# VectorE's share of a delta rule step, dealt out over the slots

## The chip, the cores and the metric

One core of a Trainium2 chip runs the whole program in one launch. The metric is the device time of one execution in microseconds (us); the number of record is the median of three executions. Beside them stands one profiled execution, whose span is the stretch that the trace covers.

## What is computed

Three blocks run one after the other on 1024 tokens of width 1024. The change touches one stage of the first block only: a bidirectional gated delta rule with 4 heads of width 128, computed in chunks. This is its core, cut short:

```python
def gated_delta_chunked(q, k, v, g, beta):
    gc = jnp.cumsum(g, axis=-1)
    gamma = jnp.exp(jnp.where(lower, gc[..., :, None] - gc[..., None, :], -jnp.inf))
    kb = k * beta[..., None]
    a_mat = jnp.where(strict, jnp.einsum('bhncd,bhnsd->bhncs', kb, k) * gamma, 0.0)
    t_mat = a_mat + jnp.eye(C)
    u = triangular_solve(t_mat, v * beta[..., None])
    w = triangular_solve(t_mat, kb * jnp.exp(gc)[..., None])
    qk = jnp.einsum('bhncd,bhnsd->bhncs', q, k) * gamma
    q_dec = q * jnp.exp(gc)[..., None]
    k_dec = k * jnp.exp(gc[..., -1:] - gc)[..., None]
    def step(S, inp):
        v_new = u_n - einsum(w_n, S)
        o = einsum(qd, S) + einsum(qk_n, v_new)
        S = S * gl + einsum(kd, v_new)
        return S, o
```

Two directions (forward and backward in time) run it, and their outputs are added. Beside it, in the same stage, the block computes a two-dimensional neighbourhood attention over 16 rows of 64 tokens, 8 heads taken as 4 pairs.

## The kernel before

The program is written engine by engine, and each engine runs its list in order; semaphores tie the lists together. The stage in question (front step `("gdn", "na", "gout")`) is a loop of slots. In every slot each engine runs first its piece of the delta rule (`gdn_pe`, `gdn_act`, `gdn_dve`), then its piece of the neighbourhood attention (`na_pe`, `na_act`, `na_dve`), then, late in the stage, a piece of the normalisation of the delta rule's output (`gout_*`).

A delta rule step n (0 to 7, a chunk of 128 tokens for each direction d) has 14 slots, s = 0 to 13; slots 10 to 13 of n = -1 come before them. An attention row takes 7 slots, so two rows fall on a step.

The slots of a step, on the engines that matter here:

- Inverse of the triangular matrix, by 7 levels. In an odd slot TensorE multiplies (`Q`, L1039) while VectorE turns the matrix block by block (`g_D`, L1235), and VectorE then masks the product (`g_gu`, L1242, semaphore `lev`). In the even slot behind it TensorE multiplies again (`X`, L1039; it waits for `lev` and `D`), and VectorE subtracts the result (`g_Dt`, L1251). Level l stands in slots 2l-1 and 2l; the last level has shapes of its own (L1049, L1238).
- Slot 0: TensorE makes the outputs of the step before (L1064, L1065) and the update of the state (L1088 by the helper's line L1033); VectorE copies the outputs (L1217, L1220) and updates the state `g_S` of both directions (L1226, 8 instructions).
- Slot 3: VectorE makes the decayed queries `g_qd` (L1256). ScalarE, in slot 4, writes beta times v over the tile `g_R` that they were made from (L1165, semaphore `vb`), so it waits for `qd`.
- Slot 6: TensorE multiplies keys by the state (`kS`); VectorE makes the right side `g_R` of both directions (L1263, 8 instructions).
- Slot 8: keys by queries on TensorE (`kq`, L1033, `ps<-g_qT,mixT` in the trace), their gates on VectorE (L1271).
- Slot 10: keys turned (L1056), which waits for `R`; slot 12: the gate rows of the next step, TensorE's `row` (L1128), then VectorE's `g_dec` (L1280) and `g_qk` (L1282), then ScalarE's exponentials (L1178).

Of the attention row, p counts its slots: a score product (L1330, bank 6) in p = 0 to 3, each followed on VectorE by the bias and maximum (`biased`, L1443), which frees the bank for the next score; exponentials (L1385) in p = 4 and 5; turned probabilities (L1338, copied by L1393); weighing (L1353) in p = 7 and 8; the square of its result on ScalarE (L1414) and sums on VectorE (L1463 to L1467) in p = 9; the scaled rows `n_z` (L1479) in p = 10; the fold on TensorE (L1378), which waits for `n_z`, in p = 11. In slot s of a step the rows stand at p = s+4 and s+11 for s under 3, s+4 and s-3 from slot 3, and s-3 and s-10 from slot 10 (p up to 11).

Of the kernel before, what the change touches and what calls it, by code (L numbers as in the profile page):

```python
# [10 lines left out]
ALU = mybir.AluOpType  # L11
# [8 lines left out]
TC = T // P  # L20
# [12 lines left out]
GH = 4  # L33
# [87 lines left out]
def build_program(nc, g):  # L121

    ctx = ExitStack()
    with ctx:
# [529 lines left out]
        g_qT = main.take("g_qT", [P, GH, T])  # L654
# [20 lines left out]
        G_LOG, G_CUM, G_TOT, G_BETA, G_NEGDEC, G_KDEC, G_LAST, G_TMP = range(8)  # L675
# [279 lines left out]
        def chunk_of(n, d):  # L955
            return n if d == 0 else TC - 1 - n

        def toks(c):
            return slice(P * c, P * c + P)

        def once(n, d):
            return 2 * n + d + 1
# [23 lines left out]
        def gbank(d, i):  # L986
            return 3 * d + i

        def pbank(b):
            return ps[:, b, :].rearrange("p (h x) -> p h x", h=GH)  # L990

        def gmask(d, j):
            return g_mask[:, d, j, :].unsqueeze(1).to_broadcast([P, GH, P])
# [5 lines left out]
        def gcol(i, n, d, h):  # L999
            return g_gates[:, i, d, chunk_of(n, d), h:h + 1]  # L1000
# [29 lines left out]
        def gdn_pe(pe):  # L1030
# [43 lines left out]
            for n, s in gdn_slots():  # L1074
# [44 lines left out]
                if s == 10 and n >= 0:  # L1119
                    for d in range(2):  # L1120
                        pe.wait_ge(gs["R"], once(n, d))
                        turned(gbank(d, 0), g_kT[:, :, toks(chunk_of(n, d))]).then_inc(gs["kt"], 1)
                if s == 12 and n + 1 < TC:
                    for d in range(2):
                        pe.wait_ge(gs["gu"], once(n + 1, d))
                        if n >= 0:
                            pe.wait_ge(gs["kd"], once(n, d))
                        nc.tensor.matmul(ps[:, gbank(d, 0), :], const("ones"), four(g_vn[d][:, :, :]), start=True, stop=True)\  # L1128
                            .then_inc(gs["row"], 1)
# [11 lines left out]
        def gdn_act(act):  # L1141
            for n, s in gdn_slots():
# [13 lines left out]
                if s == 11 and n >= 0:  # L1156
                    act.wait_ge(gs["Q"], upper(n, 1, l))
                    for d in range(2):
                        nc.scalar.activation(g_gu[d][side(d), :, side(1 - d)], pbank(gbank(d, 1))[side(d), :, side(1 - d)], ACT.Copy)\
                            .then_inc(gs["lev"], 1)  # L1160
                if s == 4 and n >= 0:
                    for d in range(2):
                        act.wait_ge(gs["qd"], once(n, d))
                        for h in range(GH):
                            ins = nc.scalar.activation(g_R[d][:, h, :], g_vt[:, chunk_of(n, d), h, :], ACT.Copy, scale=gcol(G_BETA, n, d, h))  # L1165
                        ins.then_inc(gs["vb"], 1)
# [29 lines left out]
        def gdn_dve(dve):  # L1196
# [3 lines left out]
            for n, s in gdn_slots():  # L1200
# [11 lines left out]
                if s == 0 and n:  # L1212
                    for d in both_ways(m):
# [4 lines left out]
                        else:  # L1218
                            dve.wait_ge(gs["oe"], TC)
                            nc.vector.tensor_tensor(out, out, pbank(gbank(d, 1)), ALU.add).then_inc(gs["oe"], 1)  # L1220
                if s == 0 and 0 < n < TC:
                    for d in range(2):
                        dve.wait_ge(gs["su"], once(m, d))
                        dve.wait_ge(gs["S"], once(m, d))
                        for h in range(GH):
                            ins = nc.vector.scalar_tensor_tensor(g_S[d][:, h, :], g_S[d][:, h, :], gcol(G_LAST, m, d, h),  # L1226
                                                                 pbank(gbank(d, 0))[:, h, :], op0=ALU.mult, op1=ALU.add)
                        ins.then_inc(gs["S"], 1)
                if 1 <= s <= 12 and s % 2 and n >= 0:


# [12 lines left out]
                if 1 <= s <= 12 and s % 2 == 0 and n >= 0:  # L1244
                    if l == NL - 1:
                        dve.wait_ge(gs["X"], upper(n, 1, l))
                    for d in range(2):
# [2 lines left out]
                            block = halves(g_Dt[d][:, :, :], l, 1 - d)[part, :, pairs]  # L1250
                            ins = nc.vector.tensor_tensor(block, block, halves(pbank(gbank(d, 2)), l, 1 - d)[part, :, pairs], ALU.subtract)  # L1251
                        ins.then_inc(gs["Dt"], 1)
                if s == 3 and n >= 0:
                    for d in range(2):
                        dve.wait_ge(gs["eg"], once(n, d))
                        nc.vector.tensor_tensor(g_qd[d][:, :, :], g_R[d][:, :, :], g_qT[:, :, toks(chunk_of(n, d))], ALU.mult)\  # L1256
                            .then_inc(gs["qd"], 1)
                if s == 6 and n >= 0:
                    for d in range(2):
                        dve.wait_ge(gs["kS"], once(n, d))  # L1260
                        dve.wait_ge(gs["vb"], once(n, d))
                        for h in range(GH):
                            ins = nc.vector.scalar_tensor_tensor(g_R[d][:, h, :], pbank(gbank(d, 0))[:, h, :], gcol(G_NEGDEC, n, d, h),  # L1263
                                                                 g_R[d][:, h, :], op0=ALU.mult, op1=ALU.add)
                        ins.then_inc(gs["R"], 1)
                if s == 8 and n >= 0:
                    for d in range(2):
                        dve.wait_ge(gs["kq"], once(n, d))
# [3 lines left out]
                if s == 10 and n + 1 < TC:  # L1272
                    for d in range(2):
                        nc.vector.tensor_tensor(g_vn[d][:, :, :], gmask(d, 0), gcols(G_LOG, n + 1, d), ALU.mult).then_inc(gs["gu"], 1)
                if s == 12 and n + 1 < TC:
                    for d in range(2):
                        dve.wait_ge(gs["row"], once(n + 1, d))
                        if n >= 0:
                            dve.wait_ge(gs["A"], once(n, d))
                        nc.vector.tensor_tensor(g_dec[d][:, :, :], gmask(d, 2), pbank(gbank(d, 0)), ALU.subtract).then_inc(gs["t1"], 1)  # L1280
                    for d in range(2):
                        nc.vector.tensor_tensor(g_qk[d][:, (n + 1) % 2], pbank(gbank(d, 0)), gmask(d, 1), ALU.add).then_inc(gs["t0"], 1)  # L1282
                if s == 13 and n + 1 < TC:
# [1888 lines left out]
```

## Time and profile before

| | before |
|---|---|
| median of three runs | 3978.2 us (3976.43 to 3981.91) |
| the profiled execution's own time | 3975.48 us |
| its span | 3973.7 us |
| TensorE busy, share of the span | 3842.0 us, 97% |
| VectorE busy | 2220.7 us, 56% |
| ScalarE busy | 1553.9 us, 39% |
| granted TensorE clock, mean | 0.99 |

The stage lies at about 415 to 865 us of the span. In a timeline a row gives the start, the time from the first start to the last end of the instructions merged in it, the engine, the line, and in brackets the idle time before it with what ended it. Matmuls overlap their neighbours, so the start of the next row is the better measure of what a group takes.

### The profile page before, as it was taken

How to read it: one execution, taken by the hardware profiler on the slowest of the kernel's cores; microseconds unless marked ns; L12 is line 12 of the kernel's file. 1: busy time of each engine (PE TensorE's matmuls, PEld its weight loads, DVE VectorE, ACT ScalarE, POOL GpSimd, SP SyncE). 2: the span in 40 equal slices, each digit the busy share in tenths (PEclk: the TensorE clock that was granted, in tenths of full speed). 3: DMA queues.
4: the chain of work that ended last, by engine and by line, in shares of the span. 5: the costliest groups of instructions: out<-in, count | busy, mean ns of one | idle time of the engine just before them, and what ended most of it. 6: DMA issues, size and time to landing. Idle time of an engine off the chain costs nothing.

```text
span 3973.7 us, 49060 instructions
## 1 busy us (share of the span) xinstructions
PE 3842.0 (97%) x20396; PEld 3092.6 (78%) x20396; DVE 2220.7 (56%) x3368; ACT 1553.9 (39%) x2487; POOL 17.1 (0%) x34
## 2 busy tenths in 40 slices
PE   4999999989999999999999999999999999999999
PEld 2777777777788787877778878977777877778887
DVE  6541677766534557865568646356646346545333
ACT  3351444553333434443534334233334233334333
POOL 0000000000000000000000000000000000000000
PEclk9999999999999999999999999999999999999999
DMA  4112000122332222222222222222222222223222
GB/s 170 48 59 76 10 7 14 28 93 85 96 112 96 86 95 80 80 86 90 90 80 76 96 89 87 91 85 80 80 86 93 93 85 80 80 88 114 96 96 85
DMA packets 113875, 323.55 MB, mean 81 GB/s; under 512 B 26920, under 2 KB 34040, under 8 KB 113656
## 3 DMA queue, kind: packets, MB, share of 16 engines
q1 hardware_dynamic: 111416, 314.91, 24.1%
q0 software_dynamic: 2240, 5.51, 0.7%
q8 instruction: 163, 2.67, 0.3%
q14 instruction: 56, 0.46, 0.0%
HBM read 303.86 MB, written 18.06 MB: 81 GB/s over the span
## 4 chain that ended last, share of the span: by engine, by line
PE 89%; DVE 6%; ACT 3%; issue 1%; DMA 1%; SPq 0%; DVEq 0%; ACTq 0%
PE ps L311 50%; PE ps L289 26%; PE ps L1353 2%; PE ps L727 1%; PE ps L2468 1%; PE ps L1039 1%; PE ps L1033 1%; PE ps L1330 1%; PE ps L1907 1%; PE ps L421 1%; DVE g_D L1235 1%; ACT g_dec L1178 0%; PE ps L1338 0%; ACT n_s L1385 0%; DVE a L508 0%
## 5 line engine op out<-in xcount | busy, mean ns | idle before, releaser
L311 PE MATMUL ps<-a,w_hi 128*128 128x512 f32 (+1 forms) x6128 | 1877.7, 391 | 9.4 <-DVE a L508 6.7
L311 PEld LDWEIGHTS ps<-a,w_hi 128*128 128x128 f32 x6128 | 1127.7, 189 | 284.1 <-issue 23.9
L311 PE MATMUL ps<-a,w_lo 128*128 128x512 f32 (+1 forms) x3064 | 1163.8, 386 | 0.0
L262 DVE TENSOR_TENSOR w_lo<-w_raw,w_hi 128x1024 fp32r<-128x1024 f32 x539 | 658.0, 1221 | 441.9 <-ACT w_hi L257 439.0
L257 ACT ACTIVATE w_hi<-w_raw 128x1024 fp32r<-128x1024 f32 x539 | 564.0, 1050 | 549.6 <-DMA w_raw<-in_w_mlp 343.1
L311 PEld LDWEIGHTS ps<-a,w_lo 128*128 128x128 f32 x3064 | 571.5, 189 | 122.7
L289 PE MATMUL ps<-h_hi,w_hi 128*128 128x512 f32 x1536 | 490.4, 401 | 1.9 <-DVE xT L361 1.9
L289 PE MATMUL ps<-h_hi,w_lo 128*128 128x512 f32 x1536 | 481.3, 395 | 0.0
L289 PE MATMUL ps<-h_lo,w_hi 128*128 128x512 f32 x1536 | 481.3, 395 | 0.0
L356 DVE TENSOR_TENSOR h_lo<-u_sq,h_hi 128x512 fp32r<-128x512 f32 x192 | 132.9, 692 | 498.2 <-ACT h_hi L346 498.0
L361 DVE TENSOR_TENSOR xT<-xT,ps 128x1024 f32<-128x1024 f32 x192 | 234.1, 1219 | 288.6 <-PE ps L289 287.7
L289 PEld LDWEIGHTS ps<-h_hi,w_hi 128*128 128x128 f32 x1536 | 285.8, 189 | 73.2 <-issue 5.8
L289 PEld LDWEIGHTS ps<-h_hi,w_lo 128*128 128x128 f32 x1536 | 289.7, 189 | 66.0
L289 PEld LDWEIGHTS ps<-h_lo,w_hi 128*128 128x128 f32 x1536 | 289.9, 189 | 65.7
L341 ACT ACTIVATE u_act<-ps 128x512 f32<-128x512 f32 x128 | 76.3, 596 | 368.0 <-PE ps L311 367.9
L1880 DVE SCALAR_TENSOR_TENSOR mixh<-c_pad,params,mixh 128x512 f32<-128x512 f32 x240 | 163.7, 744 | 0.0
L341 ACT ACTIVATE u_act<-ps,params 128x512 f32<-128x512 f32 x64 | 44.0, 688 | 218.4 <-PE ps L311 218.4
L345 ACT ACTIVATE u_sq<-u_act 128x512 f32<-128x512 f32 x192 | 121.3, 632 | 17.7 <-ACT u_act L341 0.4
L346 ACT ACTIVATE h_hi<-u_act 128x512 fp32r<-128x512 f32 x192 | 118.1, 615 | 0.0
L367 DVE TENSOR_TENSOR xT<-xT,ps 128x512 f32<-128x512 f32 x48 | 32.9, 686 | 137.1 <-PE ps L311 137.1
L2526 ACT ACTIVATE l_e<-l_e 128x256 f32<-128x256 f32 x56 | 23.4, 418 | 144.7 <-DVE l_e L2562 143.7
L1443 DVE CUSTOM_DVE_ANT_0 n_s<-ps,n_bias 128x512 f32<-128x512 f32 (+1 forms) x80 | 45.4, 583 | 53.3 <-PE ps L1330 52.8
(355 smaller groups left out, 3135.9 us busy)
## 6 DMA issues: line engine op xcount, KB each, us to landing
w_raw<-in_w_mlp SPq DMA_DIRECT2D x384, 512.0 KB, 3.3
w_raw<-in_w_in SPq DMA_DIRECT2D x107, 512.0 KB, 3.3
w_raw<-in_w_out SPq DMA_DIRECT2D x48, 512.0 KB, 3.3
xT<-in_x SPq DMA_DIRECT2D x2, 2048.0 KB, 12.6
x<-xT SPq DMA_DIRECT2D x2, 2048.0 KB, 7.6
xT<-x SPq DMA_DIRECT2D x2, 2048.0 KB, 10.4
rpb_rows<-in_rpb SPq DMA_DIRECT2D x1, 3810.0 KB
z<-staged SPq DMA_DIRECT2D x4, 512.0 KB, 3.7
```

The lines of the kernel that those rows point to most:

```text
L257: nc.scalar.activation(w_hi[u.z][:, :], w_raw[u.z][:, :], ACT.Copy).then_inc(w_hi_done[u.z], 1)
L262: nc.vector.tensor_tensor(w_lo[u.z][:, :], w_raw[u.z][:, :], w_hi[u.z][:, :].bitcast(F32), ALU.subtract).then_inc(w_split[u.z], 1)
L289: last = nc.tensor.matmul(ps[:, u.bank + c, :], w[:, k * 256 + c * P:k * 256 + (c + 1) * P], act[:, (u.first + k) % RING, :], start=(k == ...
L311: last = nc.tensor.matmul(ps[:, bank, 0:t1 - t0], w[:, k * P:(k + 1) * P], a[:, h, low, k, t0:t1], start=(i_k == 0 and i == 0), stop=(i_k ...
L341: nc.scalar.activation(u_act[:, s, :], ps[:, u.bank, :], ACT.Relu, bias=bias).then_inc(bank_free(u), 1)
L345: nc.scalar.activation(u_sq[:, s, :], u_act[:, s, :], ACT.Square)
L346: nc.scalar.activation(h_hi[:, u.chunk % RING, :], u_act[:, s, :], ACT.Square).then_inc(hid_hi, 1)
L356: nc.vector.tensor_tensor(h_lo[:, r, :], u_sq[:, u.chunk % 2, :], h_hi[:, r, :].bitcast(F32), ALU.subtract)\
L361: nc.vector.tensor_tensor(two, two, ps[:, u.bank:u.bank + 2, :], ALU.add).then_inc(bank_free(u), 1)
L1353: last = nc.tensor.matmul(ps[:, 7, c * P:(c + 1) * P], n_pt[c][:, t, :], v, start=(t == 0), stop=(t == KR // 2 - 1))
L1443: ins = nc.vector.tensor_tensor_reduce(n_s[:, c, t0:t1], ps[:, 6, t0:t1], bias, 1.0, -3.0e38, op0=ALU.add, op1=ALU.max, accum_out=n_small[ ...
L1880: nc.vector.scalar_tensor_tensor(y, x, w, y, op0=ALU.mult, op1=ALU.add).then_inc(c_tap, 1)
```

## The change

Of the delta rule step, the order on three engines changes; no computation is added or taken away.

- VectorE: the state update (slot 0, both directions) and the decayed queries (slot 3, both) go to slot 2 for direction 0 and slot 4 for direction 1, behind the subtraction of the level. The right side (slot 6, both) goes to slot 7 for direction 0 and slot 9 for direction 1, behind the masking of the level. `g_dec` goes from slot 12 to slot 11; `g_qk` stays in slot 12, behind the level's subtraction.
- TensorE: `row` goes from slot 12 to slot 11.
- ScalarE: beta times v goes from slot 4 to slot 5.

```diff
-                if s == 12 and n + 1 < TC:
+                if s == 11 and n + 1 < TC:
                     for d in range(2):
                         pe.wait_ge(gs["gu"], once(n + 1, d))
...
-                if s == 4 and n >= 0:
+                if s == 5 and n >= 0:
                     for d in range(2):
                         act.wait_ge(gs["qd"], once(n, d))
...
-                if s == 0 and 0 < n < TC:
-                    for d in range(2):
-                        dve.wait_ge(gs["su"], once(m, d))
-                        dve.wait_ge(gs["S"], once(m, d))
-                        for h in range(GH):
-                            ins = nc.vector.scalar_tensor_tensor(g_S[d][:, h, :], g_S[d][:, h, :], gcol(G_LAST, m, d, h),
-                                                                 pbank(gbank(d, 0))[:, h, :], op0=ALU.mult, op1=ALU.add)
-                        ins.then_inc(gs["S"], 1)
...
-                if s == 3 and n >= 0:
-                    for d in range(2):
-                        dve.wait_ge(gs["eg"], once(n, d))
-                        nc.vector.tensor_tensor(g_qd[d][:, :, :], g_R[d][:, :, :], g_qT[:, :, toks(chunk_of(n, d))], ALU.mult)\
-                            .then_inc(gs["qd"], 1)
-                if s == 6 and n >= 0:
-                    for d in range(2):
-                        dve.wait_ge(gs["kS"], once(n, d))
-                        dve.wait_ge(gs["vb"], once(n, d))
...
+                if s in (2, 4) and 0 < n < TC:
+                    d = s // 2 - 1
+                    dve.wait_ge(gs["su"], once(m, d))
+                    dve.wait_ge(gs["S"], once(m, d))
...
+                if s in (2, 4) and n >= 0:
+                    d = s // 2 - 1
+                    dve.wait_ge(gs["eg"], once(n, d))
+                    nc.vector.tensor_tensor(g_qd[d][:, :, :], g_R[d][:, :, :], g_qT[:, :, toks(chunk_of(n, d))], ALU.mult)\
+                        .then_inc(gs["qd"], 1)
+                if s in (7, 9) and n >= 0:
+                    d = s // 2 - 3
+                    dve.wait_ge(gs["kS"], once(n, d))
+                    dve.wait_ge(gs["vb"], once(n, d))
...
-                if s == 12 and n + 1 < TC:
+                if s == 11 and n + 1 < TC:
                     for d in range(2):
                         dve.wait_ge(gs["row"], once(n + 1, d))
                         if n >= 0:
                             dve.wait_ge(gs["A"], once(n, d))
                         nc.vector.tensor_tensor(g_dec[d][:, :, :], gmask(d, 2), pbank(gbank(d, 0)), ALU.subtract).then_inc(gs["t1"], 1)
+                if s == 12 and n + 1 < TC:
                     for d in range(2):
                         nc.vector.tensor_tensor(g_qk[d][:, (n + 1) % 2], pbank(gbank(d, 0)), gmask(d, 1), ALU.add).then_inc(gs["t0"], 1)
```

VectorE, slots 2 and 3 of a step, before (`g_S_108` and `g_qd_110` are direction 0's state and decayed queries, `g_S_109` and `g_qd_111` direction 1's; L1460 is the attention's reciprocal):

```order
L1251 TENSOR_TENSOR g_Dt_103<-g_Dt_103,ps 64x4x16x2 x2
L1251 TENSOR_TENSOR g_Dt_104<-g_Dt_104,ps 64x4x16x2 x2
L1460 RECIPROCAL n_small<-n_small 128x4
L1235 STREAM_TRANSPOSE g_D_101<-g_Dt_103 128x512
L1235 STREAM_TRANSPOSE g_D_102<-g_Dt_104 128x512
L1242 TENSOR_TENSOR g_gu_97<-ps,g_lev 128x64x4
L1242 TENSOR_TENSOR g_gu_98<-ps,g_lev 128x64x4
L1256 TENSOR_TENSOR g_qd_110<-g_R_105,g_qT 128x512
L1256 TENSOR_TENSOR g_qd_111<-g_R_106,g_qT 128x512
```

The same slots now; the changed kernel's lines are L1243 for the subtraction, L1227 for the turning, L1234 for the masking, L1461 for the reciprocal:

```order
L1243 TENSOR_TENSOR g_Dt_103<-g_Dt_103,ps 64x4x16x2 x2
L1243 TENSOR_TENSOR g_Dt_104<-g_Dt_104,ps 64x4x16x2 x2
L1250 SCALAR_TENSOR_TENSOR g_S_108<-g_S_108,g_gates,ps 128x128 x4
L1256 TENSOR_TENSOR g_qd_110<-g_R_105,g_qT 128x512
L1461 RECIPROCAL n_small<-n_small 128x4
L1227 STREAM_TRANSPOSE g_D_101<-g_Dt_103 128x512
L1227 STREAM_TRANSPOSE g_D_102<-g_Dt_104 128x512
L1234 TENSOR_TENSOR g_gu_97<-ps,g_lev 128x64x4
L1234 TENSOR_TENSOR g_gu_98<-ps,g_lev 128x64x4
```

Direction 0's state update and queries now stand ahead of the turning and masking of level 2; direction 1's pair stands behind the subtraction of slot 4 in the same way.

VectorE, slots 6 and 7, before (L1443, printed as ISA, is `biased` of the fourth score):

```order
L1251 TENSOR_TENSOR g_Dt_104<-g_Dt_104,ps 64x4x4x8 x2
L1263 SCALAR_TENSOR_TENSOR g_R_105<-ps,g_gates,g_R_105 128x128 x4
L1263 SCALAR_TENSOR_TENSOR g_R_106<-ps,g_gates,g_R_106 128x128 x4
L1470 TENSOR_TENSOR n_small<-n_small 128x4
L1479 TENSOR_TENSOR n_z<-ps,n_small 64x4x64 x2
L1443 ISA n_s,n_small<-ps,n_bias 128x512
L1443 ISA n_small 128x1
L1457 TENSOR_SCALAR n_small<-n_small 128x4
L1235 STREAM_TRANSPOSE g_D_101<-g_Dt_103 128x512
L1235 STREAM_TRANSPOSE g_D_102<-g_Dt_104 128x512
L1242 TENSOR_TENSOR g_gu_97<-ps,g_lev 128x16x16
L1242 TENSOR_TENSOR g_gu_98<-ps,g_lev 128x16x16
```

And now (L1471 and L1480 are the attention's two of p = 10, L1444 is `biased`, L1458 its negated maximum):

```order
L1243 TENSOR_TENSOR g_Dt_104<-g_Dt_104,ps 64x4x4x8 x2
L1471 TENSOR_TENSOR n_small<-n_small 128x4
L1480 TENSOR_TENSOR n_z<-ps,n_small 64x4x64 x2
L1444 ISA n_s,n_small<-ps,n_bias 128x512
L1444 ISA n_small 128x1
L1458 TENSOR_SCALAR n_small<-n_small 128x4
L1227 STREAM_TRANSPOSE g_D_101<-g_Dt_103 128x512
L1227 STREAM_TRANSPOSE g_D_102<-g_Dt_104 128x512
L1234 TENSOR_TENSOR g_gu_97<-ps,g_lev 128x16x16
L1234 TENSOR_TENSOR g_gu_98<-ps,g_lev 128x16x16
L1263 SCALAR_TENSOR_TENSOR g_R_105<-ps,g_gates,g_R_105 128x128 x4
```

The right side has left the place between the subtraction and `n_z`; direction 0's four instructions stand behind the masking, direction 1's four come behind the masking of slot 9.

## Rows read from the trace of the kernel before

**Rows 1.** The page: busy time, share of the span and instructions of each engine.
```profile
PE 3842.0 (97%) x20396; PEld 3092.6 (78%) x20396; DVE 2220.7 (56%) x3368; ACT 1553.9 (39%) x2487; POOL 17.1 (0%) x34
```
**Rows 2.** Waits of 465 to 860 us: who for whom, total, times, longest.
```profile
PE ps L1039 <- DVE g_gu L1242: 10.8, 16, 1.6
...
PE ps L1378 <- DVE n_z L1479: 5.8, 7, 0.8
```
**Rows 3.** Timeline of TensorE, slots 7 and 8 of step 3.
```profile
611.77 1.12 PE L1039 MATMUL ps<-g_Dt,g_A 64*64 64x32 f32 x32
613.73 1.10 PE L1378 MATMUL ps<-consts,n_z 128*128 128x64 f32 x8 [0.83 <-DVE n_z L1479]
616.18 1.12 PE L1039 MATMUL ps<-g_gu,g_D 64*64 64x32 f32 x32 [1.35 <-DVE g_gu L1242]
617.23 3.66 PE L1033 MATMUL ps<-g_qT,mixT 128*128 128x128 f32 x16
620.68 1.10 PE L1338 MATMUL ps<-consts,n_s 128*128 128x128 f32 x8
```
**Rows 4.** Timeline of VectorE, slots 6 to 8 of step 3.
```profile
610.55 2.16 DVE L1263 SCALAR_TENSOR_TENSOR g_R<-ps,g_gates,g_R 128x128 f32<-128x128 f32 x8
612.63 0.15 DVE L1470 TENSOR_TENSOR n_small<-n_small 128x4 f32<-128x4 f32 x1
...
613.70 0.69 DVE L1443 CUSTOM_DVE_ANT_0 n_s<-ps,n_bias 128x512 f32<-128x512 f32 x1
...
614.51 1.30 DVE L1235 STREAM_TRANSPOSE g_D<-g_Dt 128x512 f32<-128x512 f32 x2
615.73 0.72 DVE L1242 TENSOR_TENSOR g_gu<-ps,g_lev 128x256 f32<-128x256 f32 x2
616.88 1.20 DVE L1251 TENSOR_TENSOR g_Dt<-g_Dt,ps 64x128 f32<-64x128 f32 x4 [0.43 <-PE ps L1039]
619.22 0.69 DVE L1271 TENSOR_TENSOR g_qk<-ps,g_qk 128x512 f32<-128x512 f32 x1 [1.15 <-PE ps L1033]
```
**Rows 5.** One microsecond of step 3: busy of each engine, PEclk, DMA share, GB/s.
```profile
618.00:619.00 1.00, 1.00 (x7) 1.00 (x7) 0.07 (x1) 0.16 (x2) 0.00 (x0) 0.50 0.00 0
```
**Rows 6.** Timeline of VectorE, slots 0 to 4 of step 3.
```profile
591.01 2.15 DVE L1226 SCALAR_TENSOR_TENSOR g_S<-g_S,g_gates,ps 128x128 f32<-128x128 f32 x8 [0.20 <-PE ps L1033]
...
596.03 1.20 DVE L1251 TENSOR_TENSOR g_Dt<-g_Dt,ps 64x128 f32<-64x128 f32 x4 [1.01 <-PE ps L1039]
...
599.34 1.28 DVE L1256 TENSOR_TENSOR g_qd<-g_R,g_qT 128x512 f32<-128x512 f32 x2
...
605.60 0.69 DVE L1443 CUSTOM_DVE_ANT_0 n_s<-ps,n_bias 128x512 f32<-128x512 f32 x1 [2.08 <-PE ps L1330]
```
**Rows 7.** Timeline of TensorE, the second product of level 2, step 3.
```profile
601.60 1.12 PE L1039 MATMUL ps<-g_gu,g_D 64*64 64x32 f32 x32
```
**Rows 8.** Timelines of ScalarE (slots 4 and 5) and VectorE (slot 5), step 3.
```profile
604.74 0.77 ACT L1414 ACTIVATE n_zsq<-ps 64x256 f32<-64x256 f32 x2 [2.24 <-PE ps L1353]
...
608.14 0.41 DVE L1465 TENSOR_REDUCE n_small<-n_zsq 128x4 f32<-128x256 f32 x1
```
**Rows 9.** Timeline of TensorE, slots 7 and 8 of steps 5 and 7.
```profile
726.31 1.12 PE L1039 MATMUL ps<-g_gu,g_D 64*64 64x32 f32 x32 [0.71 <-DVE g_gu L1242]
727.36 2.05 PE L1033 MATMUL ps<-g_qT,mixT 128*128 128x128 f32 x16
...
837.34 1.92 PE L1039 MATMUL ps<-g_gu,g_D 64*64 64x32 f32 x32
839.18 3.70 PE L1033 MATMUL ps<-g_qT,mixT 128*128 128x128 f32 x16
```
**Rows 10.** Timeline of TensorE, slot 12 of step -1, the stage's start.
```profile
419.95 3.32 PE L1128 MATMUL ps<-g_vn,consts 128*128 128x512 f32 x4
```
**Rows 11.** Timelines of TensorE and ScalarE, slot 12 of step 3.
```profile
632.58 1.99 PE L1128 MATMUL ps<-g_vn,consts 128*128 128x512 f32 x4
...
634.46 2.45 ACT L1178 ACTIVATE g_dec<-g_dec,g_gates 128x128 f32<-128x128 f32 x8 [4.42 <-DVE g_dec L1280]
```

More of the change, by code:

```diff
@@ L1252, in gdn_dve @@
                         ins.then_inc(gs["Dt"], 1)
-                if s == 3 and n >= 0:
-                    for d in range(2):
-                        dve.wait_ge(gs["eg"], once(n, d))
-                        nc.vector.tensor_tensor(g_qd[d][:, :, :], g_R[d][:, :, :], g_qT[:, :, toks(chunk_of(n, d))], ALU.mult)\
-                            .then_inc(gs["qd"], 1)
-                if s == 6 and n >= 0:
-                    for d in range(2):
-                        dve.wait_ge(gs["kS"], once(n, d))
-                        dve.wait_ge(gs["vb"], once(n, d))
[L1262 to L1265, printed above, removed]
+                if s in (2, 4) and 0 < n < TC:
+                    d = s // 2 - 1
+                    dve.wait_ge(gs["su"], once(m, d))
+                    dve.wait_ge(gs["S"], once(m, d))
+                    for h in range(GH):
+                        ins = nc.vector.scalar_tensor_tensor(g_S[d][:, h, :], g_S[d][:, h, :], gcol(G_LAST, m, d, h),
+                                                             pbank(gbank(d, 0))[:, h, :], op0=ALU.mult, op1=ALU.add)
+                    ins.then_inc(gs["S"], 1)
+                if s in (2, 4) and n >= 0:
[7 more added lines that the diff above has]
+                    dve.wait_ge(gs["vb"], once(n, d))
+                    for h in range(GH):
+                        ins = nc.vector.scalar_tensor_tensor(g_R[d][:, h, :], pbank(gbank(d, 0))[:, h, :], gcol(G_NEGDEC, n, d, h),
+                                                             g_R[d][:, h, :], op0=ALU.mult, op1=ALU.add)
+                    ins.then_inc(gs["R"], 1)
                 if s == 8 and n >= 0:
```

## The prediction

> **What bounds the kernel now.** Read the busy shares first: TensorE is busy for 97% of the span, VectorE for 56% [rows 1]. So time can only be won where TensorE stands still or runs at its lower clock, and work that is moved on VectorE matters only where TensorE waits for it. The second view is the list of waits in the stage: TensorE waits for VectorE's `g_gu` 16 times, 10.8 us in all, and for `n_z` 7 times, 5.8 us [rows 2]. The third is the timeline of one step, which shows that nearly all of this lies in slots 7 and 8. TensorE ends the first product of level 4 and waits 0.83 us for `n_z` before the fold, then 1.35 us for the masked product before the second one [rows 3]. On VectorE the cause stands ahead of both: the right side, 8 instructions from 610.55 to 612.63, thus 2.08 us, with `n_z`, `biased` and the level's turning queued behind it [rows 4].
>
> A second loss follows from that one. The keys by queries behind the two gaps take 3.66 us [rows 3], at a granted clock of 0.50 [rows 5], which is 1.2 GHz. In step 5 the same 16 instructions take 2.05 us [rows 9]: there the gap ahead of the second product is 0.71 us, since a product of the output's normalisation fills part of it. So the idle 2.2 us of slots 7 and 8 is followed by a lower clock and 1.6 us more, in steps 0 to 4.
>
> **Slots 6 to 8, the right side leaves.** Without it the small multiply at 612.63 starts at 610.55 and `n_z` ends 2.1 us sooner, before TensorE comes to the fold: the 0.83 us wait goes. `biased` at 613.70 could start 2.08 us sooner, at 611.6, but its score leaves TensorE only at about 611.8 (the next product starts at 611.77 [rows 3]), so it starts near 611.9. That is 1.8 us sooner, and the turning (614.51), the masking (615.73) and TensorE's second product (616.18) follow in a fixed chain: 616.18 becomes 614.4. TensorE has ended the fold by 613.7, so some 0.6 us of idle time stays, in place of 2.2. I take 1.8 us a step here.
>
> **The clock of slot 8.** With 0.6 us of idle time the state of step 5 (0.71 us in one piece ahead of the product, 2.05 us for the keys by queries) is the nearest row, so I take the higher level: 3.66 less 2.05 is 1.6 us a step in steps 0 to 4. Step 7 is slow although it has the filling product: its second product of level 4 takes 1.92 us and the keys by queries 3.70 [rows 9], against 1.12 and 2.05, so 0.8 and 1.65 us, 2.4 in all, are there to be had. The bounds are nothing and all of it, together 5 x 1.6 + 2.4 = 10.4 us.
>
> The page "TensorE: Matmul & The Clock Gate" of the Trainium skill (part 1, what is actually happening) says that the throttled state is the default, that activity releases it, and that what watches the activity is free-running, so that the same code can meet it at different points. Steps 5 and 7 here agree: nearly the same order and gaps, one fast and one slow. By the page the low clock could come back somewhere in a step by chance; that is the first rival below.
>
> **What the right side meets in slots 7 and 9.** Call the start of the second product of level 4 t. VectorE then does direction 0's right side (1.04 us) from t + 0.25, the subtraction (1.20), two gates of 0.69 (until t + 3.8), the turning (614.51 to 615.73, 1.22) and half the masking (0.36): ready at t + 5.4 [rows 4]. TensorE meanwhile does this product (1.05), keys by queries (1.9 at the full clock), two turns of 1.04 (620.68 on [rows 3]) and the first product of level 5 (1.05): 6.1 us. Margin 0.65 us, so no new wait; the first product of level 5 needs the second gate at t + 3.8 and starts at t + 4.0. Direction 1's 1.04 us lies behind the masking of slot 9, ends about t + 6.7, and the turned keys that wait for it start about t + 7.1. In steps 5 and 7, and in step 6, normalisation adds to VectorE and leaves a gap ahead of level 5 as it does now; I keep it.
>
> **Slots 2 and 4, the state and the queries.** From slot 0 goes 2.07 us, from slot 3 1.28 us [rows 6]. None of it is waited for there: behind slot 0 VectorE is idle 1.01 us before its subtraction (596.03), and behind the queries it waits for a score. So nothing is won. What comes in: 1.07 + 0.64 = 1.7 us behind the subtraction in slot 2. The masking of level 2 ended at 599.34, where the queries started; now it ends at 601.0. The product that waits for it starts at 601.60 [rows 7]. Cost nothing, with 0.6 us of cover; past that it costs TensorE one for one. In slot 4 the other 1.7 us goes into the 2.08 us for which VectorE waited at 605.60 [rows 6]: cost nothing, cover 0.4 us.
>
> **Slot 5, beta times v.** ScalarE's first direction can start once slot 2's queries are done, the second (1.2 us) at about 605.2. The square behind it moves from 604.74 to about 606.5 and ends by 607.3; VectorE reads it at 608.14 [rows 8]. Cost nothing, cover 0.8 us. The right side needs `vb` only from slot 7.
>
> **Slots 11 and 12, the gate rows.** `row` (1.82 us) moves ahead of the weighing, and all of TensorE stands behind it if it waits; it needs `kd` of ScalarE, which ends some 1.4 us before. `g_dec` goes into VectorE's wait for the second score. ScalarE's exponentials, now held 4.42 us for `g_dec` [rows 11], start sooner and no longer hold up the square and the sums of slot 12. TensorE loses `row` as cover between the second and the third score, a gap of 0.2 us, and gains the 0.2 us that the fourth score waits now. Sum: nothing. At the start of the stage (n = -1) `row` runs 3.32 us at the lower clock, behind a wait [rows 10], and now stands ahead of the second score, where TensorE is idle anyway: 1 to 3 us won, I take 2.
>
> **The sum.** Slots 7 and 8: 8 steps x 1.8 = 14.4. Clock: 10.4. Start: 2. Together 26.8; less 0.3 for the clock that step 4 shares partly, 26.5 us. The profiled execution's own 3975.5 us would become 3949.0. The median of the runs shown is 2.7 us above it, so the forecast is 3978.2 - 26.5 = 3951.7. Nothing behind the stage is late on its own: its loads start when the last weighing is done, and shift with it.
>
> **Rivals.**
> First, the idle time goes and the clock doesn't come back: the low clock falls behind another gap, such as the new 0.6 us, the 0.2 us of slot 12 or the normalisation's. For it: step 7. Against: steps 5 and 6 with more idle time than I forecast. Then 26.5 - 10.4 = 16.1 us are won: 3962.
> Second, the wait moves on: slots 8 to 10 are short by their 0.65 us of cover, the level 5 product waits for turning and masking, and gives back the 1.8 us of each step. What is left is little more than the start: about 3975. For it: VectorE is the engine waited for in all of this stage. Against: the sum of slot 8 above.
> Third, slower: the chain of VectorE through slots 2 to 5 becomes the bound. Its covers are the thinnest, 0.6 and 0.4 us. If both pairs were waited for in full, 3.4 us a step would be added, 8 x 3.4 = 27 us, against 16 won without the clock: 3978.2 + 27 - 16 = 3989. It decides from the point where the pair of slot 2 ends over 0.6 us later than worked out, and it makes the kernel slower only when more than 2 us a step are uncovered. Against: the durations are measured on the same instructions, and nothing that the pair waits for is late.
> That the change would not do what it says is no rival: the order of the built kernel shows the moves.
>
> **Chances.** The forecast, 3946 to 3956: 0.66. First rival, 3956 to 3966: 0.22. Second, the rest up to no change: 0.08. Third: 0.04. 0.2% is 8 us, about what a measurement of this kernel can tell from no change. Faster by more than that takes in the first two, 0.88; within it 0.07; slower 0.05. The range goes from 32 us won (3 at the start, the small waits of 0.2 us gone too) at 3945, to the first rival with 2 us less, 3964.
>
> **What would show it.** In slots 7 and 8 the fold should have no idle time ahead of it and the second product about 0.6 us; the keys by queries should take 2.05 us in all steps; a step should last 51.1 us in place of 54.6. The level 2 product should still have no wait, the level 5 one none in steps 0 to 4. The waits of TensorE for `n_z` should be gone. Keys by queries of 3.66 us would mean the first rival, idle time ahead of level 5 in every step the second, idle time ahead of level 2 the third. What would make it wrong altogether is a wait that these rows don't show: ScalarE's exponentials of the attention row, which now have less of TensorE's work ahead of the turns in slot 8.

## The result

| | before | changed |
|---|---|---|
| median | 3978.35 us (3976.43 to 3981.91, 4 runs) | 3948.72 us (3948.34 to 3949.23, 4 runs) |
| span of the profiled execution | 3973.7 us | 3946.6 us |
| TensorE busy | 3842.0 us | 3829.4 us |

The ratio is 0.9925, with a 95% interval of 0.9907 to 0.9942: the change saves 29.6 us by the medians and 27.1 us by the two spans. The forecast was 26.5 us and 3951.7 us. Of the kernel with the turning ahead of the bias, further below, one execution took 6123 us at a mean granted clock of 0.579, and its median is that of the other three.

The waits of TensorE in the stage, changed kernel, 458 to 840 us (waiting engine and line, what it waited for, total, times, longest); the line numbers have moved by a few, `n_z` is now L1480 and the masking L1234:

```profile
PE ps L1039 <- DVE g_gu L1234: 5.7, 14, 0.7
PE ps L1379 <- DVE n_z L1480: 5.2, 1, 5.2
```

They answer to [rows 2]. The waits for `n_z` inside the steps are gone; the one that is left, 5.2 us, is that of the stage's end, which the window of [rows 2] didn't reach (before, it was 4.8 us). The waits for the masking fell from 10.8 to 5.7 us.

TensorE, slots 7 and 8 of step 3, which answer to [rows 3]:

```profile
598.38 1.12 PE L1039 MATMUL ps<-g_Dt,g_A 64*64 64x32 f32 x32
599.43 1.10 PE L1379 MATMUL ps<-consts,n_z 128*128 128x64 f32 x8
600.96 1.12 PE L1039 MATMUL ps<-g_gu,g_D 64*64 64x32 f32 x32 [0.42 <-DVE g_gu L1234]
602.01 2.05 PE L1033 MATMUL ps<-g_qT,mixT 128*128 128x128 f32 x16
603.90 1.04 PE L1339 MATMUL ps<-consts,n_s 128*128 128x128 f32 x8
```

The fold follows the first product without a gap. The second product starts 2.58 us after the first one, where it was 4.41 us, so 1.83 us are saved. The keys by queries take 2.05 us in place of 3.66. VectorE in the same slots, to be read beside [rows 4]:

```profile
595.93 1.20 DVE L1243 TENSOR_TENSOR g_Dt<-g_Dt,ps 64x128 f32<-64x128 f32 x4
597.16 0.16 DVE L1471 TENSOR_TENSOR n_small<-n_small 128x4 f32<-128x4 f32 x1
597.36 0.86 DVE L1480 TENSOR_TENSOR n_z<-ps,n_small 64x256 f32<-64x256 f32 x2
598.49 0.69 DVE L1444 CUSTOM_DVE_ANT_0 n_s<-ps,n_bias 128x512 f32<-128x512 f32 x1 [0.28 <-PE ps L1331]
...
599.30 1.30 DVE L1227 STREAM_TRANSPOSE g_D<-g_Dt 128x512 f32<-128x512 f32 x2
600.52 0.72 DVE L1234 TENSOR_TENSOR g_gu<-ps,g_lev 128x256 f32<-128x256 f32 x2
601.16 1.11 DVE L1263 SCALAR_TENSOR_TENSOR g_R<-ps,g_gates,g_R 128x128 f32<-128x128 f32 x4
```

The chain is now released by the fourth score (idle 0.28 us), and the right side stands behind the masking.

The lengths of the steps add up to the whole. From one step's keys by queries to the next one's, before and after, in us:

| step to step | before | changed | saved |
|---|---|---|---|
| first score to step 0 | 38.22 | 33.14 | 5.08 |
| 0 to 1 | 54.45 | 52.28 | 2.17 |
| 1 to 2, 2 to 3 | 54.54, 54.56 | 51.01, 51.01 | 3.53, 3.55 |
| 3 to 4 | 55.30 | 51.55 | 3.75 |
| 4 to 5 | 54.83 | 51.68 | 3.15 |
| 5 to 6 | 55.51 | 53.74 | 1.77 |
| 6 to 7 | 56.31 | 53.74 | 2.57 |
| step 7 to the last fold | 26.11 | 24.82 | 1.29 |
| the stage | 449.83 | 422.96 | 26.87 |

The stage is counted from the start of its first score product to the start of its last fold. What is outside the stage is 0.88 us shorter ahead of it and 0.65 us longer behind it, with the same code. Behind the stage the profiled executions of all the kernels below differ by 3.5 us (3105.6 to 3109.1), so the stage tells small differences better than the span does.

### The profile page after: what moved, and what is told of

It reads as the page before. It is cut to its first block, busy times and chain, and to the rows that moved or that the text cites. A ratio compares the mean times of both kernels' runs of the same rounds, so it can differ in the third digit from the quotient of the medians.

```text
span 3946.6 us, 49060 instructions
## 1 busy us (share of the span) xinstructions
PE 3829.4 (97%) x20396; PEld 3084.1 (78%) x20396; DVE 2220.5 (56%) x3368; ACT 1553.3 (39%) x2487; POOL 17.1 (0%) x34
## 4 chain that ended last, share of the span: by engine, by line
PE 91%; DVE 5%; ACT 2%; issue 1%; DMA 1%; SPq 0%; DVEq 0%; ACTq 0%
PE ps L311 50%; PE ps L289 26%; PE ps L1033 2%; PE ps L1354 2%; PE ps L1039 1%; PE ps L1331 1%; PE ps L727 1%; PE ps L2469 1%; PE ps L1908 1%; PE ps L421 1%; PE ps L1339 0%; DVE g_D L1227 0%; ACT n_s L1386 0%; PE ps L1128 0%; DVE n_s L1444 0%
## 5 line engine op out<-in xcount | busy, mean ns | idle before, releaser
L1331 PE MATMUL ps<-n_k,n_zq 128*128 128x512 f32 (+2 forms) x160 | 68.2, 524 | 2.9 <-DVE n_small L1444 2.1
```

The source lines that it names most:

```text
L1331: last = nc.tensor.matmul(ps[:, 6, t0:t1], n_zq[k % 2][:, c, :], n_k[:, c, row * GRID:row * GRID + t1 - t0], start=True, stop=True)
```

## Experiments

Two theories were tested. Theory A is the prediction's: the right side in slot 6 holds up the chain to the fold and to level 4, its idle time brings the lower clock, and the other moves lie in idle time except at the start. Theory B: the spreading as a whole makes the gain, or the covers are other than worked out. Since totals move by some us with the place where the clock falls (see below), each run is read by its stage too, by the number of steps whose keys by queries took more than 3 us ("slow steps"), and by the length of an undisturbed step. The numbers are those of one profiled execution of each kernel, taken on several chips.

| kernel | span | stage | slow steps | a step |
|---|---|---|---|---|
| before | 3973.7 | 449.83 | 6 | 54.55 |
| changed | 3946.6 | 422.96 | 1 | 51.01 |
| right side only | 3949.3 | 425.31 | 0 | 51.10 |
| all but the right side | 3967.0 | 443.84 | 5 | 54.46 |
| gate rows only | 3964.4 | 444.19 | 5 | 54.47 |
| state and queries only | 3973.6 | 449.77 | 6 | 54.55 |
| right side, both in 7 | 3949.3 | 427.12 | 1 | 51.55 |
| four added in 6 | 3955.0 | 431.67 | 2 | 51.81 |
| eight added in 6 | 3969.0 | 446.06 | 6 | 54.4 |
| eight added in 2 | 3958.7 | 434.01 | 2 | 52.2 |
| turning ahead of the bias | 3948.4 | 422.47 | 1 | 50.91 |
| and normalisation later | 3951.5 | 427.91 | 2 | 50.91 |
| only slot 8's normalisation later | 3942.7 | 421.32 | 1 | 51.01 |
| and half a turning, the maximum | 3941.2 | 417.38 | 0 | 50.71 |

### The right side alone

The kernel before, with this part of the change alone:

```diff
-                if s == 6 and n >= 0:
-                    for d in range(2):
-                        dve.wait_ge(gs["kS"], once(n, d))
-                        dve.wait_ge(gs["vb"], once(n, d))
...
+                if s in (7, 9) and n >= 0:
+                    d = s // 2 - 3
+                    dve.wait_ge(gs["kS"], once(n, d))
+                    dve.wait_ge(gs["vb"], once(n, d))
```

> The kernel before with one part of the change: the right side in slots 7 (direction 0) and 9 (direction 1); state, decayed queries, beta times v and gate rows stay where they were. Theory A (the right side in slot 6 is the whole of the cause, and its idle time brings the lower clock with it): 8 x 1.8 us of waits and about 10 us of clock go, about 3952 us; keys by queries take 2.05 us in steps 1 to 7. Theory B (the spreading matters as a whole; the state and the queries taken from slots 0 and 3 carry a part): less than half of the gain, 3965 us or more.

Measured: 3952.4 us (3951.1 to 3953.4) against 3975.4 for the kernel before on the same chip; ratio 0.9946, interval 0.9931 to 0.9960. The stage is 24.5 us shorter, of the 26.9 of the whole change, and no step is slow. Theory A holds: by the stage this part carries nine tenths. That share is a little flattered, since no step was slow here and one was in the changed kernel.

### Everything but the right side

The changed kernel with the right side put back into slot 6.

> The changed kernel with the right side put back into slot 6, both directions. Theory A: only the start of the stage is won, 2.5 us, so about 3976 us, with 0.83 and 1.35 us of idle time in slots 7 and 8 and keys by queries of 3.66 us. Theory B: a third to a half of the gain stays, 3963 to 3969 us.

Measured: 3969.9 us, ratio 0.9987 (0.9977 to 0.9996), so 5.5 us less than before in place of 2.5. TensorE in slots 7 and 8 of step 3 is as it was:

```profile
609.70 1.10 PE L1379 MATMUL ps<-consts,n_z 128*128 128x64 f32 x8 [0.83 <-DVE n_z L1480]
612.15 1.12 PE L1039 MATMUL ps<-g_gu,g_D 64*64 64x32 f32 x32 [1.34 <-DVE g_gu L1234]
613.20 3.15 PE L1033 MATMUL ps<-g_qT,mixT 128*128 128x128 f32 x16
```

Both waits and the slow product are back; a step takes 54.46 us. What goes beyond the expectation lies in two places: 2.4 us in step 7, whose products run at the full clock here, with the same gap of 0.84 us ahead of its fold, and 1.0 us at the start of step 0, which belongs to the gate rows (next experiment). So theory A is right on the steps, and its sum for this kernel was short by one fall of the clock and by part of what the start is worth. The parts of the change do not add up (24.5 and 6.0 us of the stage against 26.9), since the full clock at the start and in step 7 came with either of them.

### The gate rows alone, the state and the queries alone

The kernel before, with `row` and `g_dec` in slot 11; and the kernel before, with the state update and the queries in slots 2 and 4 and beta times v in slot 5.

```diff
-                if s == 12 and n + 1 < TC:
+                if s == 11 and n + 1 < TC:
                     for d in range(2):
                         pe.wait_ge(gs["gu"], once(n + 1, d))
```

> The kernel before with the gate rows alone moved (row product and g_dec in slot 11). Theory A: the first step's turning of A starts 2.5 us earlier against the stage's start, and the steps behind it last as long as before: a step of 54.5 us. Theory B: ScalarE's earlier exponentials shorten each step, by up to 0.4 us.

> The kernel before with the state update and the decayed queries dealt out over slots 2 and 4 and beta times v in slot 5. Theory A: no step gets shorter or longer (54.5 us), since what leaves slots 0 and 3 was not waited for and what comes into slots 2 and 4 lies in idle time. Theory B: steps shorter by 1 us or more.

The gate rows: the start, on TensorE:

```profile
414.65 1.10 PE L1331 MATMUL ps<-n_k,n_zq 128*128 128x512 f32 x2 [0.83 <-issue]
416.23 1.98 PE L1128 MATMUL ps<-g_vn,consts 128*128 128x512 f32 x4 [0.48 <-DVE g_vn L1274]
418.05 1.02 PE L1331 MATMUL ps<-n_k,n_zq 128*128 128x512 f32 x2
419.87 1.12 PE L1331 MATMUL ps<-n_k,n_zq 128*128 128x512 f32 x2 [0.79 <-DVE n_small L1444]
```

From the first score to the turning of the first matrix there are 8.83 us in place of 11.35, as expected: 2.5 us. The row product takes 1.98 us where [rows 10] shows 3.32. Another 1.0 us comes behind it, in slots 1 to 3 of step 0: from the first product of level 1 to that of level 4 it takes 18.23 us in place of 19.24, and TensorE's waits for ScalarE's exponentials and copies there, 0.32 and 0.28 us, are gone. All kernels with the gate rows in the new place have the shorter stretch in step 0 (18.2 us, and 18.8 with the eight instructions in slot 2); the three with them in the old place have 19.2 to 19.6. So the gate rows are worth 3.5 us at the start. A later step takes 54.47 us, 0.08 less than before, so there the earlier exponentials bring next to nothing. The stage is 5.6 us shorter, since step 7 was not slow in this run either. Whether the moved row product or chance spares step 7 stays open: it was spared in this kernel and in that with everything but the right side, and slow in the run with eight instructions added in slot 6, which has the gate rows in the new place as well.

The state and the queries: stage 449.77 against 449.83 us, a step 54.55 us, the same 6 slow steps. These moves are worth nothing, as the prediction said. Both kernels had one timed run, at 3966.2 and 3975.4 us.

### Both directions of the right side in slot 7

```diff
-                if s in (7, 9) and n >= 0:
-                    d = s // 2 - 3
+                if s == 7 and n >= 0:
+                    for d in range(2):
```

> The changed kernel with both directions' right side in slot 7 (8 instructions, 2.08 us, ahead of the subtraction of level 4). It measures the cover of slots 8 to 10, which the prediction put at 0.65 us. Theory A: direction 1's 1.04 us goes ahead of a chain with 0.65 us of cover, so the first or second product of level 5 waits 0.4 to 0.9 us in a step, 3 to 7 us in all. Theory B (the cover is larger): no new wait, same span as the change.

TensorE then waits for the first of VectorE's two gates ahead of the first product of level 5:

```profile
606.21 1.25 PE L1039 MATMUL ps<-g_Dt,g_A 64*64 64x32 f32 x32 [0.34 <-DVE g_qk L1271]
```

A step takes 51.55 us, 0.54 more, and the stage 4.2 us more (3951.1 us in one run). Of the 1.04 us that were put ahead, 0.5 were covered. It is the gates that come late, ahead of the first product, and not the turning and masking ahead of the second one, for which the prediction had worked out 0.65 us; for the gates it had 0.2 us (t + 3.8 against t + 4.0). Theory A holds, and dealing the right side out over two slots rather than one is worth these 4 us.

### Idle time and clock apart

Useless instructions of the right side's kind, four and eight, in slot 6 of the changed kernel:

```diff
+                if s == 6 and n >= 0:
+                    for i in range(8):
+                        d, h = i // GH, i % GH
+                        nc.vector.scalar_tensor_tensor(g_dec[d][:, h, :], g_dec[d][:, h, :], gcol(G_LAST, n, d, h),
+                                                       g_dec[d][:, h, :], op0=ALU.mult, op1=ALU.add)
```

> The changed kernel with four useless instructions of the right side's kind on VectorE in slot 6 (they rescale a tile that is overwritten before it is read), some 1.04 us. It separates idle time from clock. Theory A: the second product of level 4 comes about 0.9 us later (part of the 1.04 us hides in VectorE's wait for the score of 0.28 us), idle time 1.2 to 1.3 us in slots 7 and 8; the clock holds, so keys by queries stay at 2.05 us; 7 us longer than the change. Theory B (the clock goes lower with each added gap): keys by queries over 3 us in steps 1 to 4 too, 14 us longer.

> The changed kernel with eight such instructions in slot 6, some 2.08 us, as much as the right side took there. Theory A: idle time of 2.2 us and keys by queries of 3.66 us come back with it, 24 to 27 us longer than the change, 14 of them idle time. Theory B: idle time comes back but the clock doesn't, 14 us longer; then it was something else about the right side that lowered the clock.

With eight, all comes back, TensorE in step 3:

```profile
608.97 1.10 PE L1384 MATMUL ps<-consts,n_z 128*128 128x64 f32 x8 [0.86 <-DVE n_z L1485]
611.42 1.12 PE L1039 MATMUL ps<-g_gu,g_D 64*64 64x32 f32 x32 [1.34 <-DVE g_gu L1234]
```

The stage is 23.1 us longer than in the change (theory A: 24 to 27), and 6 steps are slow. So the work in that place is the cause, whatever it computes. With four (`range(4)` in the same place), step 1 and step 3 show the same order and the same gap, and differ:

```profile
503.92 1.12 PE L1039 MATMUL ps<-g_gu,g_D 64*64 64x32 f32 x32 [1.22 <-DVE g_gu L1234]
...
607.54 1.12 PE L1039 MATMUL ps<-g_gu,g_D 64*64 64x32 f32 x32 [1.22 <-DVE g_gu L1234]
```

Step 1's keys by queries take 2.05 us, step 3's 3.27. The granted clock around step 3's, in stretches of two microseconds (length of the stretch, busy time of the engines, then the clock, DMA share and GB/s):

```profile
606.00:608.00 2.00, 0.78 (x19) 0.64 (x18) 2.00 (x6) 1.64 (x4) 0.00 (x0) 1.00 0.19 43
608.00:610.00 2.00, 2.00 (x33) 1.96 (x30) 1.90 (x8) 1.65 (x6) 0.00 (x0) 0.79 0.00 0
610.00:612.00 2.00, 2.00 (x11) 2.00 (x11) 0.78 (x2) 0.00 (x0) 0.00 (x0) 0.50 0.00 0
```

TensorE was idle for 1.22 of the first two microseconds, at the full clock, and its clock fell to half behind it, while it was busy. The fall came in steps 0 and 3, and not in steps 1 and 2 with the same gap, nor in step 4 with 1.52 us, nor in steps 5 to 7, where 0.6 us are left. Theory A said never, theory B every time; both are wrong in part. The wait is 0.80 us more a step, as theory A had it, and the stage 8.7 us longer.

### The cover of slot 2

The same eight instructions behind the state and the queries of slot 2.

> The changed kernel with eight such instructions behind the state and the queries of slot 2, some 2.08 us. It measures the cover of slot 2 (the prediction's third rival). Theory A: cover 0.6 to 0.8 us, so the second product of level 2 waits 1.3 to 1.5 us in each step, 11 us longer, and the clock may fall behind it. Theory B (the cover is thicker): under 4 us longer.

Measured, TensorE in slot 4 of step 3:

```profile
594.64 1.12 PE L1039 MATMUL ps<-g_gu,g_D 64*64 64x32 f32 x32 [1.06 <-DVE g_gu L1234]
```

The instructions take 2.10 us on VectorE, and TensorE waits 1.06 us: 1.0 us were covered, not 0.6. The stage is 11.0 us longer, two slow steps among them. The prediction counted the cover to the end of both directions' masking; TensorE begins with the first direction's, which in the changed kernel is done at 587.2, 1.0 us ahead of the product at 588.21.

### Shorter still

In the first of these runs the turning of level 4 goes ahead of the fourth bias; in the second the normalisation goes from slots 8 and 1 to 10 and 3.

```diff
+                    if p == 3 and (i - 4) % 14 == 6 and i >= 4:
+                        for d in range(2):
+                            dve.wait_ge(gs["Dt"], level((i - 4) // 14, d, 3))
+                            nc.vector.transpose(four(g_D[d][:, :, :]), four(g_Dt[d][:, :, :])).then_inc(gs["D"], 1)
                     if p < 4:
                         biased(k, p)
```

> The changed kernel with VectorE's turning of level 4 taken from slot 7 to slot 6, between n_z and the bias of the fourth score, so that it no longer lies between that score and the masked product. Theory A (the 0.42 us left ahead of the second product of level 4 is this chain): the idle time goes in all steps, 8 x 0.42 to 0.7, about 3 us, and the clock fall of step 0, 1.5 us: 3944 to 3946 us. Theory B (n_z or the fold is late, and takes the wait over): no gain, 3948 us or more.

> The kernel of the run before, and the output's normalisation on VectorE moved from slots 8 and 1 to slots 10 and 3. Theory A: the idle time of 0.74 us ahead of the second product of level 5 in steps 5, 6 and 7 goes as well, another 2.2 us: about 3942 us. Theory B: it comes back in slot 10 or 3 as a wait for the subtraction, same as the run before.

Neither gained. With the turning early the gap ahead of the second product is 0.32 us in place of 0.42: the 1.22 us of turning now push the bias itself past the score that released it (it starts 1.19 us behind the start of the level's first product, where it was 0.11), and only 0.1 of the 0.28 us of idle time turned into gain. Median 3950.3 us, ratio 0.9935 (0.9915 to 0.9955). With the normalisation later, median 3952.3 us, ratio 0.9939 (0.9925 to 0.9954), a new wait stands in slot 4 of steps 6 and 7:

```profile
753.41 1.19 PE L1333 MATMUL ps<-n_k,n_zq 128*128 128x448 f32 x4 [0.81 <-DVE n_small L1446]
```

The piece in slot 3 stands ahead of the first bias, and the second score waits for that. The wait of 0.74 us ahead of level 5 did go. So the next two runs took what had worked. First the changed kernel with only slot 8's normalisation moved:

```diff
-                if at == 8:
+                if at == (8 if i % 2 else 10):
                     pieces.append(("norm", i))
```

> The changed kernel with only the normalisation of slot 8 moved to slot 10 (that of slot 1 stays). In the run with both moved the piece in slot 3 held up the first bias and lost 0.81 and 0.34 us a step. Theory A: the 0.74 us ahead of the second product of level 5 go in steps 5 to 7, 2.2 us, and nothing new comes: steps 5 and 6 of 50.9 and 53.0 us in place of 51.7 and 53.7; 3946 to 3947 us. Theory B: the subtraction or the gate of slot 10 is held up, steps as long as in the change. Where the clock falls differs by up to 3 us from run to run and blurs the total; the steps decide.

Then, on top of it, one direction's turning ahead of the bias, and the negated maximum behind the masking:

```diff
+                    if p == 3 and i >= 4 and (i - 4) % 14 == 6:
+                        dve.wait_ge(gs["Dt"], level((i - 4) // 14, 0, 3))
+                        nc.vector.transpose(four(g_D[0][:, :, :]), four(g_Dt[0][:, :, :])).then_inc(gs["D"], 1)
                     if p < 4:
                         biased(k, p)
...
+                if s == 7 and n >= 0:
+                    negated(dve, 2 * n + 1)
```

> The kernel of the run before, and in slot 6 direction 0's turning of level 4 ahead of the fourth bias (0.61 us, 0.28 of it in VectorE's wait for the score), with the negated maximum of that row moved behind the masking of slot 7 (0.2 us). Theory A: the chain from the fourth score to the masked product gets 0.28 + 0.2 us shorter, so the 0.42 us ahead of the second product of level 4 goes in steps 0 to 3 and most of 0.70 us in step 4: a step of 50.6 us in place of 51.0, 2 us in all. Theory B: the gain is as small as with both directions turned early, 0.1 us a step.

The first: 3944.7 us (3943.7 to 3950.6), ratio 0.9921 (0.9906 to 0.9936); steps 5 to 6 and 6 to 7 last 52.92 and 52.93 us, 0.8 less. The second: 3942.9 us (3938.3 to 3943.2), ratio 0.9910 (0.9893 to 0.9926); a step takes 50.71 us. In steps 0 to 3 its slots 7 and 8 have no gap left (0.23 us stay in step 4); step 3:

```profile
597.18 1.12 PE L1039 MATMUL ps<-g_Dt,g_A 64*64 64x32 f32 x32
598.23 1.10 PE L1383 MATMUL ps<-consts,n_z 128*128 128x64 f32 x8
599.47 1.12 PE L1039 MATMUL ps<-g_gu,g_D 64*64 64x32 f32 x32
600.53 2.05 PE L1033 MATMUL ps<-g_qT,mixT 128*128 128x128 f32 x16
```

Its stage is 5.6 us shorter than the change's, some 1.6 of them because no step was slow in this execution. The intervals of the two ratios against the kernel before overlap, so that it beats the changed kernel rests on the steps and on medians 5.8 us apart, taken on different chips.

## Why the prediction was right, point by point

- **Where the loss was.** Right: slots 7 and 8, held up by the right side. Taking it away alone brings 24.5 of 26.9 us; putting equal work in its place takes back 23.1.
- **1.8 us a step of waits.** Measured 1.83 in step 3. The second product starts where it was forecast, 2.6 us behind the first one. The idle time ahead of it is 0.42 us and not 0.6, because the fold ends 2.15 us behind the start of the first product, where the forecast had it at 1.9. In steps 5 to 7, where a product of the normalisation stands between, 1.7 us were saved and no idle time is left.
- **The clock, 10.4 us.** Mechanism right, size nearly. Steps 1 to 4 gave 1.63, 1.63, 1.61 and 1.36 us on keys by queries, step 7 3.1 in all, with 0.65 us on the normalisation's product; that makes 9.6. The 0.65 us stand where steps 5 and 6 wait 0.7 us, so the forecast had them among the waits. Step 0 gave only 0.3: there the clock fell again, behind a gap of 0.42 us. The claim that 0.6 us of idle time keeps the clock because 0.71 had done so in step 5 was too plain. In this execution it held in four of the five steps with such a gap, and that was in part luck: step 4, with 0.70 us, kept the clock here, but over all the traces it lost it in four of seven kernels with one gap of 0.61 to 0.70 us there (last section).
- **Slots 2, 4 and 5 at no cost.** Right: alone they change the stage by 0.06 us. The covers were 1.0 us in slot 2 (forecast 0.6) and 0.33 us in slot 4, the wait that VectorE still has there (forecast 0.4).
- **Slots 7 to 10 at no cost.** Right. The masking of level 5 is ready 0.65 us ahead of its product, as forecast; what runs out first are the gates, with 0.5 us a step.
- **Gate rows.** In the steps a gap of 0.18 us came where 0.2 was forecast, and one as large went; 0.08 us a step were won. The start was mis-sized: 3.5 us in place of 2, of which 2.5 up to the turning of the first matrix and 1.0 in slots 1 to 3 of step 0, where the forecast put nothing. Some 1.7 of the 2.5 are the clock: in the run with the right side alone the start had the old order and took 9.66 us, 1.7 less than before, with its row product at 1.88 us.
- **A step of 51.1 us.** Measured 51.01.
- **The sum.** Stage 26.9 us against 26.5. That it agrees so well is partly luck, as misses cancel: slots 7 and 8 with their clock gave 23.1 us in place of 24.8, the start 1.5 us more than forecast, the gate rows 0.6 us over the steps, and 0.4 us went into the end of the stage. The medians differ by 29.6, since the median of before lies 2.9 us above its profiled execution and that of the changed kernel 0.4.
- **The rivals.** The first (the clock doesn't come back) happened in one step of eight, and in the other kernels that have the gap of 0.42 us in none to two. The second and the third did not; their mechanisms exist, at 0.5 and 1.0 us of cover, as the runs with both directions in slot 7 and with eight instructions in slot 2 show.

## What to carry to other kernels

Where one engine is the bound, look for the place at which it waits, and take out of the chain to it the work that no one there waits for; spreading work that lies in idle time anyway brings nothing. Count the cover to the first thing that the bound engine needs, and move a piece only as far as the idle time that is there: 1.22 us moved into 0.28 us of idle time gained 0.1, half of it together with one small instruction closed the gap in the steps where it was 0.42 us. An idle gap of TensorE can cost twice, once as the wait and once through the lower clock behind it.

## What the runs showed of the hardware

The place of a fall of TensorE's clock isn't settled by the code of the step. The changed kernel has the same order and the same 0.42 us gap in steps 0 and 1, and only the first is followed by the lower clock:

```profile
446.36 1.44 PE L1039 MATMUL ps<-g_gu,g_D 64*64 64x32 f32 x32 [0.42 <-DVE g_gu L1234]
447.72 3.31 PE L1033 MATMUL ps<-g_qT,mixT 128*128 128x128 f32 x16
...
498.95 1.12 PE L1039 MATMUL ps<-g_gu,g_D 64*64 64x32 f32 x32 [0.42 <-DVE g_gu L1234]
500.00 2.05 PE L1033 MATMUL ps<-g_qT,mixT 128*128 128x128 f32 x16
```

The traces of all fourteen kernels together, counted by the idle time of TensorE in slots 7 and 8 (fall: keys by queries of more than 3 us):

| idle time in slots 7 and 8 | steps | with a fall |
|---|---|---|
| none | 28 | 0 |
| one gap, 0.23 to 0.32 us | 9 | 1 |
| one gap, 0.42 us | 20 | 3 |
| one gap, 0.61 to 0.70 us, step 4 | 7 | 4 |
| one gap, 0.60 to 0.61 us, steps 5 to 7 | 3 | 0 |
| one gap, 1.22 to 1.52 us | 5 | 2 |
| 0.84 to 0.88 us ahead of the fold, up to 0.71 ahead of the second product, the normalisation's product between, steps 5 to 7 | 15 | 3 |
| two gaps with the fold between, 0.82 to 0.87 and 1.31 to 1.62 us, steps 0 to 4 | 25 | 25 |

So the two long gaps of the kernel before are followed by the lower clock every time, no gap in no case, and what lies between looks like chance. Each kernel gives one execution here, and one of the falls at 0.42 us had a gap of 1.06 us in slot 4 ahead of it as well. A fall elsewhere, as in slot 4 of step 6 of the kernel with the normalisation later, is not counted. The Trainium skill says in "TensorE: Matmul & The Clock Gate", part 1, that what watches the activity is free-running; these rows agree with that and don't prove it.

The largest gap of the stage is at its end: all fourteen traces have 4.7 to 6.3 us of idle time ahead of the last fold, in or right behind which the granted clock falls to 0.50, and it stays there for 7 to 11 us. No run here changes that.

The falls show in the spread of the times too: thirteen runs of the kernel before on one chip took 3968.9 to 3981.2 us, the shortest at a mean granted clock of 0.993 and the longest at 0.989. That a kernel with fewer gaps is steadier isn't shown: the four runs of the changed kernel lay within 0.9 us, but those of the kernel with one normalisation moved within 6.9, and those of the kernel with the fewest gaps within 4.9. One fall cost 1.1 to 2.4 us where the rows show it, so a difference of 3 us between two runs of such a kernel may be one or two falls of the clock.
